# A late update of the prompt's state and an early transpose of the embedding input in a two-layer streaming encoder

## The reference

```python
x = x + 0.5 * swiglu(rmsnorm(x, norm_g[i, 0]), ffn_w_gu[i, 0], ffn_w_d[i, 0])
x = x + mixer_i(rmsnorm(x, norm_g[i, 1]))
x = x + 0.5 * swiglu(rmsnorm(x, norm_g[i, 2]), ffn_w_gu[i, 1], ffn_w_d[i, 1])
xg = rmsnorm(x, norm_g[i, 3])
x = x + (p[i] @ w_ple[i]) * sigmoid(xg @ w_ple_gate[i])
```

```python
S = exp(gL) * S + k_end.T @ u        # the state that the chunk leaves
```

## Time and profile before

| | |
|---|---|
| three runs, us | 2697.48, 2698.7, 2701.79 (median 2698.7) |
| the profiled execution, us | 2701.65; its span of instructions 2699.9 |
| PE busy | 2658.3 us, 98% of the span |
| DVE, ACT, POOL busy | 69%, 40%, 20% |
| DMA | 205.57 MB, 76 GB/s in the mean |
| mean granted clock of TensorE | 0.993 of full speed |

### The profile page before, as it was taken

How to read it: one execution, slowest core, us unless ns; L and a number is a source line. 1 busy time by engine, 2 the same in 40 slices (tenths; PEclk the granted TensorE clock), 3 DMA queues, 4 the chain that set the end, 5 groups by cost and what they waited for, 6 DMA issues and landing times.

```text
span 2699.9 us, 43696 instructions
## 1 busy us (share of the span) xinstructions
PE 2658.3 (98%) x18213; PEld 2619.9 (97%) x18213; DVE 1863.3 (69%) x2179; ACT 1068.7 (40%) x1558; POOL 529.4 (20%) x251
## 2 busy tenths in 40 slices
PE   9999999999999999999999999999999999999998
PEld 9999999999998799999999999999999999999998
DVE  7748386987677778476577974848666786584756
ACT  5425253243222545344345552524411254252545
POOL 2130303332010030302113202030333311102041
PEclk9999999999999899999999999999999999999999
DMA  4222223232003222223232232232222223232231
GB/s 134 83 73 85 79 75 90 58 78 55 17 9 87 75 67 79 79 78 94 64 90 69 82 91 71 81 92 75 85 79 77 63 79 94 63 96 66 82 101 50
DMA packets 401149, 205.57 MB, mean 76 GB/s; under 512 B 15555, under 2 KB 398940, under 8 KB 400953
## 3 DMA queue, kind: packets, MB, share of 16 engines
q1 hardware_dynamic: 400746, 202.70, 26.4%
q10 hardware_dynamic: 206, 0.08, 0.0%
HBM read 195.14 MB, written 7.60 MB: 75 GB/s over the span
## 4 chain that ended last, share of the span: by engine, by line
PE 55%; DVE 8%; ACT 1%; issue 1%; POOL 0%; DVEq 0%; ACTq 0%
PE ps L928 9%; PE ps L929 9%; PE ps L930 9%; PE ps L913 9%; PE ps L917 9%; PE ps L914 9%; DVE ut L2203 1%; DVE x L2937 1%; DVE sumsq L2302 1%; DVE r L2388 1%; DVE hf L2810 1%; DVE x L3123 0%; PE ps L1203 0%; DVE wlo L2219 0%; DVE hl L2291 0%
## 5 line engine op out<-in xcount | busy, mean ns | idle before, releaser
L861 POOL TENSOR_TENSOR wlo<-raw,whi 128x1024 fp32r<-128x1024 f32 (+2 forms) x214 | 518.0, 2424 | 2131.4 <-ACT whi L1632 2131.2
L913 PE MATMUL ps<-xh,whi 128*128 128x320 f32 x1552 | 472.3, 312 | 7.9 <-POOL wlo L861 5.7
L914 PE MATMUL ps<-xl,whi 128*128 128x320 f32 x1552 | 467.2, 309 | 0.0
L913 PE MATMUL ps<-hh,whi 128*128 128x320 f32 x1440 | 437.7, 312 | 4.1 <-POOL wlo L861 1.8
L914 PE MATMUL ps<-hl,whi 128*128 128x320 f32 x1440 | 435.0, 310 | 0.0
L928 PE MATMUL ps<-tau_hi,whi 128*128 128x320 f32 x1280 | 396.4, 310 | 2.9 <-DVE wlo L2219 2.0
L930 PE MATMUL ps<-tau_hi,wlo 128*128 128x320 f32 x1280 | 395.5, 309 | 0.0
L929 PE MATMUL ps<-tau_lo,whi 128*128 128x320 f32 x1280 | 395.5, 309 | 0.0
L1632 ACT CAST whi<-raw 128x1024 fp32r<-128x1024 f32 (+2 forms) x216 | 208.3, 966 | 390.9 <-PE ps L917 352.0
L917 PE MATMUL ps<-xh,wlo 128*128 128x320 f32 x1552 | 353.6, 309 | 0.0
L917 PE MATMUL ps<-hh,wlo 128*128 128x320 f32 x1440 | 329.1, 310 | 0.0
(11 more groups left out here) (434 smaller groups left out, 4817.0 us busy)
## 6 DMA issues: line engine op xcount, KB each, us to landing
raw<-in_ffn_w_gu SPq DMA_DIRECT2D x320, 256.0 KB, 3.8
raw<-in_ffn_w_d SPq DMA_DIRECT2D x64, 512.0 KB, 4.0
raw<-in_w_in_even SPq DMA_DIRECT2D x32, 512.0 KB, 4.0
raw<-in_ffn_w_d SPq DMA_DIRECT2D x32, 384.0 KB, 3.6
raw<-in_w_in_odd SPq DMA_DIRECT2D x24, 512.0 KB, 3.7
raw<-in_ffn_w_gu SPq DMA_DIRECT2D x16, 512.0 KB, 4.5
raw<-in_w_ple_gate SPq DMA_DIRECT2D x16, 512.0 KB, 3.9
raw<-in_w_out_even SPq DMA_DIRECT2D x8, 512.0 KB, 4.2
```

The lines of the kernel that those rows point to most:

```text
L861: pool.tensor_tensor(ring(wlo, n), raw[:, slot, 0:kt, :], ring(whi, n).bitcast(fp32), ALU.subtract).then_inc(lo_ready, 1)
L913: pe.matmul(ps[j % 4][:, c, 0:HT], wh[:, k], hi[:, k, cs], start=(k == 0), stop=False)
L914: pe.matmul(ps[j % 4][:, c, 0:HT], wh[:, k], lo[:, k, cs], start=False, stop=False)
```

## The change

Two things are moved; nothing is added to the arithmetic, and nothing taken away.

**The prompt's state.** `keep_state` moves from behind the first level of the samples' tile to behind the third. PE gets a wait on it (`core["up"]`) ahead of the state products of head 2, since these write the bank that `keep_state` reads.

**The embedding input.** The two pT jobs are created ahead of the down blocks instead of behind block 1. PE transposes them where the filler was, behind the first five k-groups of block 0; the two filler k-groups go back to block 1. DVE turns them into high and low parts ahead of block 0 instead of behind block 1. The load of `pstage` is issued from the same place as before.

```diff
@@ ffn_stage @@
+                if last and f == 1:
+                    s["pT"] = [job("pT") for _ in range(KP)]
                 for o in range(KD):
                     blk((dn, o * P, j0 * P), cnt, "down")
-                    if last and f == 1 and o == 1:
-                        s["pT"] = [job("pT") for _ in range(KP)]
@@ sample_tile on PE @@
                 for h in range(HA):
                     if h == HA // 2:
                         sample_part("vt")
+                        pe.wait_ge(core["up"], t)
@@ the down stage on PE @@
                         if late and o == 0:
                             mm(s["n0"], *s["hid"], first=hidden, part=(0, kt - 1))
-                            mm(s["n0"] + 1, *s["hid"], part=(0, 2))
+                            if "pT" in s:
+                                pe.wait_ge(p_loaded, 32 * (s["layer"] + 1))
+                                for q, j in enumerate(s["pT"]):
+                                    tposes(j, ...)
+                            else:
+                                mm(s["n0"] + 1, *s["hid"], part=(0, 2))
                             mm(s["n0"], *s["hid"], first=hidden, part=(kt - 1, kt))
-                        elif late and o == 1:
+                        elif late and o == 1 and "pT" not in s:
                             mm(s["n0"] + 1, *s["hid"], part=(2, kt))
                         else:
                             mm(s["n0"] + o, *s["hid"], first=hidden if o == 0 else None)
-                        if o == 1 and "pT" in s:
...
@@ sample_tile on DVE @@
                 own(dve.tensor_tensor(W(7), W(7), heads(1), ALU.subtract).then_inc(core["xr"], 1), core["xr"])
-                keep_state(t - 1, gcol)
...
                 dve.wait_ge(core["d"], li + 3)
                 own(dve.tensor_tensor(W(7), W(7), heads(1), ALU.subtract).then_inc(core["xr"], 1), core["xr"])
+                keep_state(t - 1, gcol)
                 mul(W(5), heads(5), W(5))
@@ the down stage on DVE @@
                 elif kind == "down":
+                    for q, j in enumerate(s.get("pT", [])):
+                        done(j)
...
+                        free(j)
                     for o in range(KD):
...
-                        if o == 1 and "pT" in s:
...
```

More of the change, by code:

```diff
@@ L1539, in _ @@
                             mm(s["n0"], *s["hid"], first=hidden, part=(0, kt - 1))
-                            mm(s["n0"] + 1, *s["hid"], part=(0, 2))
+                            if "pT" in s:
+                                pe.wait_ge(p_loaded, 32 * (s["layer"] + 1))
+                                for q, j in enumerate(s["pT"]):
+                                    tposes(j, [(t // 4, t % 4 * P, pstage[:, t, q * P:(q + 1) * P]) for t in range(NTILE)])
+                            else:
+                                mm(s["n0"] + 1, *s["hid"], part=(0, 2))
                             mm(s["n0"], *s["hid"], first=hidden, part=(kt - 1, kt))
-                        elif late and o == 1:
+                        elif late and o == 1 and "pT" not in s:
                             mm(s["n0"] + 1, *s["hid"], part=(2, kt))
@@ L1545, in _ @@
                             mm(s["n0"] + o, *s["hid"], first=hidden if o == 0 else None)
-                        if o == 1 and "pT" in s:
-                            pe.wait_ge(p_loaded, 32 * (s["layer"] + 1))
-                            for q, j in enumerate(s["pT"]):
-                                tposes(j, [(t // 4, t % 4 * P, pstage[:, t, q * P:(q + 1) * P]) for t in range(NTILE)])
                 elif kind == "even_in":
@@ L2929, in _ @@
                 elif kind == "down":
+                    for q, j in enumerate(s.get("pT", [])):
+                        done(j)
+                        for c, z in ((0, slice(0, SEQ)), (1, slice(SEQ, T))):
+                            w = z.stop - z.start
+                            high, low = s["hid"]
+                            o1(dve.tensor_copy(high[:, PH + q, z], ps[j % 4][:, c, 0:w]))
+                            sm = h_ready if c else dve_own
+                            own(dve.tensor_tensor(low[:, PH + q, z], ps[j % 4][:, c, 0:w], high[:, PH + q, z].bitcast(fp32),
+                                                  ALU.subtract).then_inc(sm, 1), sm)
+                        free(j)
                     for o in range(KD):
@@ L2952, in _ @@
                         pair_ahead(s["n0"] + o)
-                        if o == 1 and "pT" in s:
-                            for q, j in enumerate(s["pT"]):
-                                done(j)
-                                for c, z in ((0, slice(0, SEQ)), (1, slice(SEQ, T))):
-                                    w = z.stop - z.start
-                                    high, low = s["hid"]
-                                    o1(dve.tensor_copy(high[:, PH + q, z], ps[j % 4][:, c, 0:w]))
-                                    sm = h_ready if c else dve_own
-                                    own(dve.tensor_tensor(low[:, PH + q, z], ps[j % 4][:, c, 0:w], high[:, PH + q, z].bitcast(fp32),
-                                                          ALU.subtract).then_inc(sm, 1), sm)
-                                free(j)
                 elif kind == "even_in":
```

## The result

The changed kernel takes 2704.93 us (median of 16 executions, 2700.78 to 2710.58); the kernel before, timed with it, 2699.85 us (16 executions, 2697.48 to 2703.16). The ratio is 1.0017, interval 1.0011 to 1.0023: slower by 0.17%, with an interval that reaches a little above 0.2%. The forecast was 2699.2 us, +0.5 us against before. So the case "within 0.2%" and the range came true, but the measured difference is +5.1 us between the medians, and the sum lacked 4.6 us of it, nine tenths of the loss.

What follows compares the result with a forecast made beforehand. PE, busy 98% of the span, was taken to bound the kernel. Layer 0 +0.25, layer 1 +1.0 and the state -0.75 us gave +0.5 us on the 2698.7 us median: 2699.2 us, range 2694.5 to 2706 us.

Steps and rivals of the forecast that it cites:

- the stall: Last down stages, both layers: block 0 waits for DVE's sum over X, starting 2.94 us later than before.
- what goes: Layer 0's last down stage: PE's waits for low weights from POOL, 1.29 us once, and smaller ones at emb blocks disappear.
- the state's part: Samples' tile: moving the state's four DVE instructions lets the levels run earlier, -0.75 us, bounds 0 and -1.50.
- Rival 4: Samples' tile: the state's update brings nothing, as another wait replaces it; +1.25 us, 2700 us; chance 0.08.
- rival 3: Last down stages: block 0 does not wait and the small waits go; -5.4 us, 2693.3 us; chance 0.05.
- layer 1: Last down stage of layer 1: fourth emb block starts at 2616.26 instead of 2615.25, +1.0 us.
- layer 0: Last down stage of layer 0: the stall is nearly paid by waits that go; first gate block +0.25 us.
- the last cover: Layer 0's down stage: low weights ready in time, gate block's with 0.6 us spare; failure adds some tenths.
- rival 1: Down stages: the clock falls behind the new stalls, making the kernel slower; chance 0.17 in full, 0.12 in small form.
- full form: Clock falls behind both down-stage stalls, 2.5 to 4.75 us each; +5.5 to +10 us, 2704 to 2709 us; chance 0.17.
- small form: Down stages: a shorter clock fall, or one of two, costs 1.5 to 3 us; chance 0.12.
- the sum as it stands, or within 2 us of it: Whole kernel: the terms' +0.5 us holds, or the time lies within 2 us of it; chance 0.50.

Runs made afterwards that it cites:

- the input alone: The changed kernel with the state's update put back behind the first level, so only the embedding input is moved: 2704.08 us, ratio 1.0013 against the kernel before.
- the part done alone: The kernel before with only keep_state moved behind the third level, plus PE's wait: 2701.0 us, ratio 0.9998.
- its own slot: The changed kernel with pT jobs numbered behind block 0, which keeps the free slot: 2698.46 us, then 2698.36 us; ratios 0.9991 and 0.9989 against before.
- the filled stall: The changed kernel with 17 unread products of 320 columns in each of the two stalls: 2702.62 us, ratio 1.0003 against before.
- the longer one: The changed kernel with block 0 of the two last down stages also waiting for the last hidden tile: 2712.98 us, ratio 1.0040.
- the other two timings: The unmodified changed kernel timed again against the kernel before: 2703.0 against 2700.74 us (ratio 1.0013), and 2705.63 against 2701.66 us (1.0011).
- the slot alone: The kernel before, order of work kept, with block 0, block 1 and transposes numbered as if transposes came first: 2726.01 us, ratio 1.0094.
- the first profile: The profiled execution of the changed kernel from its first timing, against 2701.65 us for the profiled one before: 2702.77 us.

## Why the prediction came out as it did

**Right: the stall.** Block 0 waits for the sum over X in both layers, from the order of the jobs alone. Predicted 2.94 us against the old start. The old start, moved by the 0.86 us won ahead of it, would be 1393.06; block 0 came at 1395.92, 2.86 us later (2.69 us of it idle, since the pair's last products end 0.17 us behind it). The rest is mostly the hand-over, 0.06 us instead of the 0.15 that I took from another pair of instructions.

**Right: what goes.** No wait for POOL is left between block 0 and the gate block of layer 0, pT is transposed in time and the load of pstage is not waited for. PE's new wait among the state products is zero.

**Right in its cause, a little too large: the state's part**, -0.75 predicted, -0.62 in the levels of the tile and -0.63 to -0.67 as the difference of the changed kernel and the input alone. The -0.77 of the part done alone holds some difference between executions. Where I took L2559 to start at 867.85, it starts at 868.09 behind 0.53 us of waiting for PE. Rival 4 falls, since the state's part is there; rival 3 falls, since block 0 waits.

**Right: layer 1**, +1.0 predicted, +1.10 measured.

**Mis-sized: layer 0**, +0.25 predicted, +1.07 measured. The failing step is the last cover: "the gate block's, ready near 1443.2, has 0.6". I counted 4.3 us from x to the low weights for every block. But the gate block's weights are not paced by x. Their high part takes the place of block 7's, so ACT's cast waits until PE has ended block 7, at 1439.51; the cast takes 1.05 us and POOL's 1024 columns 2.93 us, done at 1443.66. From the end of block 7 to the gate block are 4.25 us, and PE has only two emb blocks, 3.52 us, in between. That leaves the wait of 0.73 us, nearly all of what the term lacked. It goes with PE: the traces of the changed kernel, of the input alone, of its own slot (cast at 1435.78, gate block at 1439.95), of the filled stall and of the longer one all have 0.73 or 0.74 us, wherever the stage begins. In the kernel before the gate block was bound by POOL too, with 0.31 us of wait:

```profile
1441.07 2.39 POOL L861 TENSOR_TENSOR wlo<-raw,whi 128x1024 fp32r<-128x1024 f32 x1
```

It ends at 1443.46, 0.09 us ahead of the gate block; the rows name "issue", and I did not take it for a wait for weights. The same instruction took 2.39 us there; why it took 2.93 after is open. So time that PE wins between block 7 and the gate block is lost again there, while time won ahead of the stage is kept. The text said "some tenths" if this failed; it was eight.

**Mis-sized: the clock.** This is the larger part. Of the 4.6 us that the sum lacked (5.1 between the medians of the first timing, 0.5 given) the terms read from the traces explain about 1, and the table gives 2 to 3 that go with the mean clock; the medians of the other two timings differ by less, 2.3 and 4.0 us. The step was the chance, not the mechanism: I had named it as rival 1, gave its full form 2.5 to 4.75 us for each stall at 0.17, and its small form ("a shorter fall, or one of two, would cost 1.5 to 3 us") at 0.12, and left it out of the sum. Of its two forms the small one is what the traces show: 1.45, 1.54 and 1.55 us for each of three falls. They explain 1.1 us in the mean of four traces; what the rest of the clock's part is stays open. That the measured 2704.93 us lies where the full form put it, at 2704 to 2709, is no proof of that form. The price of the full form came from a fall of 9.5 us over narrow products; behind a stall with wide products on both sides it lasts 3.5 us. And "the sum as it stands, or within 2 us of it", at 0.50, was much too sure, since it held only if the stalls hardly ever brought the clock down. That the time still fell into the range owes to the room that it had above the sum, and is in part luck. A mean over the cases would have carried it: two stalls, at even odds and 1.5 us each, are 1.5 us in the sum.

**Not seen in time:** the stall was avoidable by numbering alone. Its own slot shows what the change is worth without it: -2.3 and -3.0 us in the two timings, and 3.0 to 3.4 us at equal mean clock. The waits of PE in the profiles give most of it: in layer 0 1.29, 0.55 and 0.31 us before and 0.74 with its own slot, in layer 1 0.49 and 1.07 before and 0.50 and 0.45 now, and the state's 0.63. Together that is 2.65 us.

## What to carry to other kernels

When jobs take buffers in turn by their number, moving one job gives all the later ones another buffer: list for each who freed it last and when, for the moved job and for every one behind it (2.69 us here, 8.60 us in the slot alone). The place in the order and the slot can be chosen apart. A new stall of a few us in dense products should be priced at its length and a part of a clock fall; look for the fall in more than one profile. When a conversion of weights waits for PE to free their place, its time counts from there and not from the data (0.73 us here). And sort timed executions by their mean clock before comparing them, which made 1.2 us visible under a spread of 10.

## What the runs showed of the hardware that was not expected

- The same pause of 2.69 us between products of 320 columns is followed by the lower clock level in one execution and not in the next: none in the first profile, one in layer 0 alone, two in another. With 5.23 and 6.22 us of pause both fell, and the level changed during the pause.
- In the six traces with this pause, falls behind it came in the three that also have a fall at 940 us, some 450 us earlier, and in none of the three without.
- Such a fall ends after about 3.5 us of dense products (3.60 and 3.70 us windows hold it whole) and costs 1.45 to 1.55 us; behind the longer pauses it costs 2.1 and 2.3. Over the narrow products of the samples' tile the clock is at the lower level for 20.5 us before and for about 30 us (870 to 910) in the first profile after.
- PE followed DVE's freeing of a slot by 0.06 us (1395.86 to 1395.92), less than half of the 0.15 us by which it followed a DVE result in the samples' tile.
- With products that nobody reads in the place of the stall, the clock stayed whole in the one profile and none of 12 executions took over 2704.6 us.
- POOL took 2.39 us for a subtraction of 1024 columns before and 2.93 us for the same one after.
